# A decoder layer with product-key experts: picks turned at step 14, blocks from step 11, the choice's places and keys in PSUM, half of the first layer norm in PSUM

## The reference, cut to what matters

```python
def reference(x, mem, ...):            # x (1, 512, 1024), one layer
    h = _hybrid_mixer(x, ...)          # gated heads | short convolution, then w_out
    x = _layernorm(ALPHA * x + h, ln1_g, ln1_b)
    h = _cross_attention(x, mem, ...)  # 4 heads over 256 memory tokens
    x = _layernorm(ALPHA * x + h, ln2_g, ln2_b)
    h = _peer(x, ...)
    return _layernorm(ALPHA * x + h, ln3_g, ln3_b)

def _peer(x, w_query, sub_keys, w_down, w_up):      # 128 x 128 experts, each one neuron
    q = (x @ w_query) -> (512 tokens, 8 heads, 2, 128)
    sc = einsum('thpk,hpnk->thpn', q, sub_keys)
    va, ia = top_k(sc[:, :, 0], 16); vb, ib = top_k(sc[:, :, 1], 16)
    top, flat = top_k(va[..., :, None] + vb[..., None, :], 16)   # 16 of the 256 pairs
    expert = ia[flat // 16] * 128 + ib[flat % 16]
    gate = softmax(top)
    act = gelu(sum_d w_down[expert] * x)
    return sum_k gate * act * w_up[expert]
```

## Time and profile before

| | |
|---|---|
| median of 3 runs | 1678.34 us (1678.11 to 1678.65) |
| profiled execution | 1678.76 us, its span 1676.9 us |
| PE, PEld | 93%, 83% of the span busy |
| DVE, ACT, POOL | 73%, 37%, 47% |
| mean granted PE clock | 0.965 of full speed |
| bytes moved | 410.80 MB, 245 GB/s over the span |
| front block, scores, down tiles up to the Gelu of tile 127, up tiles and end | 0 to 396, 396 to 520, to 1134, to 1677 us |

### The profile page before, as it was taken

The page is one execution under the profiler, slowest core; times in us unless marked ns, Lnnn a source line. Parts: engine busy times, 40 slices in busy tenths (PEclk is TensorE's granted clock), DMA queues, the critical chain, the costliest instruction groups (busy, mean ns, idle before and its releaser), DMA issues.

```text
span 1676.9 us, 22738 instructions
## 1 busy us (share of the span) xinstructions
PE 1557.5 (93%) x8252; PEld 1387.2 (83%) x8252; DVE 1218.1 (73%) x2298; ACT 626.2 (37%) x807; POOL 787.0 (47%) x460
## 2 busy tenths in 40 slices
PE   7999979897999879996999699999999999999995
PEld 6787857675889879996999699998888888888884
DVE  2544270416999988887988797468888888888887
ACT  4223232322224326632663366333333333333331
POOL 7443454041345777777768777852222222222220
PEclk9999989897999889998999899999999999999997
DMA  8422222113225768797779777998999999999992
GB/s 290 172 95 80 100 101 91 35 50 151 89 75 177 241 213 270 245 390 301 266 243 406 296 254 262 371 364 319 345 334 345 334 339 337 336 342 331 346 379 85
DMA packets 140232, 410.80 MB, mean 245 GB/s; under 512 B 15200, under 2 KB 49248, under 8 KB 139616
## 3 DMA queue, kind: packets, MB, share of 16 engines
q1 hardware_dynamic: 97072, 253.86, 43.1%
q0 software_dynamic: 36864, 134.23, 22.4%
q10 hardware_dynamic: 6192, 21.32, 3.3%
HBM read 363.22 MB, written 46.14 MB: 244 GB/s over the span
## 4 chain that ended last, share of the span: by engine, by line
PE 56%; DVE 17%; DMA 2%; issue 1%; POOL 0%; ACT 0%; DVEq 0%; ACTq 0%
PE ps L1239 10%; PE ps L1241 10%; PE ps L1240 10%; PE ps L927 7%; PE ps L928 7%; PE ps L929 7%; DVE rows L1259 2%; DMA rows<-in_w_down,expert 2%; PE ps L1211 1%; PE ps L1213 1%; DVE gmat L650 1%; DVE gmat L643 1%; DVE ab L733 1%; DVE gb L724 1%; DVE gmat L644 1%
## 5 line engine op out<-in xcount | busy, mean ns | idle before, releaser
L1119 ACT ACTIVATE w_hi<-raw 128x1024 fp32r<-128x1024 f32 x252 | 266.3, 1057 | 346.3 <-PE ps L1241 322.3
L927 PE MATMUL ps<-b_hi,w_hi 128*128 128x384 f32 x1024 | 349.2, 341 | 8.0 <-POOL w_lo L1086 8.0
L1086 POOL TENSOR_TENSOR w_lo<-raw,w_hi 128x1024 fp32r<-128x1024 f32 x119 | 287.9, 2421 | 121.4 <-ACT w_hi L1119 120.4
L928 PE MATMUL ps<-b_lo,w_hi 128*128 128x384 f32 x1024 | 344.6, 337 | 0.0
L929 PE MATMUL ps<-b_hi,w_lo 128*128 128x384 f32 x1024 | 344.5, 336 | 0.0
L1094 POOL DMA_INDIRECT rows<-in_w_up,expert x128 | 139.3, 1088 | 388.4 <-DVE ps L1293 370.9
L1239 PE MATMUL ps<-w_hi,b_hi 128*128 128x512 f32 x768 | 298.8, 389 | 0.7 <-ACT act_t L1125 0.7
L1241 PE MATMUL ps<-w_hi,b_lo 128*128 128x512 f32 x768 | 298.8, 389 | 0.0
L1240 PE MATMUL ps<-w_lo,b_hi 128*128 128x512 f32 x768 | 298.8, 389 | 0.0
L183 POOL TENSOR_TENSOR w_lo<-raw,w_hi 128x1024 fp32r<-128x1024 f32 x60 | 152.0, 2544 | 202.0 <-ACT w_hi L211 202.0
L1300 DVE TENSOR_TENSOR w_lo<-raw,w_hi 128x1024 fp32r<-128x1024 f32 x133 | 163.0, 1225 | 87.8 <-ACT w_hi L1119 87.8
(11 more groups left out here) (217 smaller groups left out, 2467.8 us busy)
## 6 DMA issues: line engine op xcount, KB each, us to landing
raw<-in_down_t SPq DMA_DIRECT2D x128, 512.0 KB, 4.0
raw<-in_up_t SPq DMA_DIRECT2D x128, 512.0 KB, 5.2
raw<-in_units SPq DMA_DIRECT2D x76, 512.0 KB, 3.2
act_d<-act_t SPq DMA_DIRECT2D x128, 192.0 KB, 5.2
c<-act_d SPq DMA_DIRECT2D x128, 192.0 KB, 5.4
gate_d<-gmat ACTq DMA_DIRECT2D x32, 512.0 KB, 15.1
v<-gate_d SPq DMA_DIRECT2D x16, 512.0 KB, 6.7
i<-gate_d SPq DMA_DIRECT2D x16, 512.0 KB, 6.5
```

Source lines behind the costliest of these rows:

```text
L927: nc.tensor.matmul(out, ring.w_hi[:, s, w], b_hi[:, c, 0:DT], start=c == 0, stop=False)
L928: nc.tensor.matmul(out, ring.w_hi[:, s, w], b_lo[:, c, 0:DT], start=False, stop=False)
L1086: nc.gpsimd.tensor_tensor(w_lo[:, s, :], raw[:, s, :], w_hi[:, s, :].bitcast(F32), ALU.subtract).then_inc(split_done, 1)
L1119: nc.scalar.activation(w_hi[:, u % W4, :], raw[:, u % W4, :], ACT.Copy).then_inc(hi_done, 1)
```

## The change

It has four parts. The first layer norm keeps blocks 0 and 1 in their PSUM banks (sum, statistics and the first operation; the second writes `xres` as before), and DVE makes the low parts of blocks 0 and 1 before the layer norm of block 3. `top_experts` writes the places and a copy of the keys of its block into PSUM bank 5, after a wait for ACT's last read of that bank, and L724 and L729 read one operand there. `LEAD` goes from 9 to 11 and `TURN_TILE` from 12 to 14 (so blocks begin two tiles later, and the picks are turned two tiles later within a block), while the gate rounds stay at steps 16 to 31. Gathers stand one step behind the dot that frees their slot in all steps. The write of `numbers` moves behind the first gates.

```diff
@@ -457,12 +457,19 @@
                 step.up(nc.vector.tensor_tensor(rc[:, 0:n], rc[:, 0:n], nt[:, 0, 0:n], ALU.mult))
                 done()
 
-            def layer_norm(u0, full, turn, ready, order):
+            def layer_norm(u0, full, turn, ready, order, in_bank=(), after=lambda b: None):
+
+                def banks(b):
+                    return ps[:, 2 * b:2 * b + 2, :]
+
+                def wide(x):
+                    return x.rearrange("p (i c) -> p i c", i=2)
 
                 def statistics(b, ready):
                     dve.wait_ge(res_added, ready)
                     for h in range(2):
-                        step.up(nc.vector.bn_stats(bst[:, 2 * b + h, :], xres[:, b, h * HALF:(h + 1) * HALF]))
+                        step.up(nc.vector.bn_stats(bst[:, 2 * b + h, :], ps[:, 2 * b + h, :] if b in in_bank else
+                                                   xres[:, b, h * HALF:(h + 1) * HALF]))
 
                 for i, b in enumerate(order):
                     if i < TB - 1:
@@ -471,7 +478,8 @@
                         dve.wait_ge(unit_done, u0 + KC)
                     for h in range(2):
                         c = slice(h * HALF, (h + 1) * HALF)
-                        added.up(nc.vector.scalar_tensor_tensor(out=xres[:, b, c], in0=xres[:, b, c], scalar=ALPHA,
+                        added.up(nc.vector.scalar_tensor_tensor(out=ps[:, 2 * b + h, :] if b in in_bank else
+                                                                xres[:, b, c], in0=xres[:, b, c], scalar=ALPHA,
                                                                 in1=ps[:, 2 * b + h, :], op0=ALU.mult, op1=ALU.add))
                     if i:
                         statistics(order[i - 1], added.n - 2)
@@ -483,12 +491,14 @@
                 dve.wait_ge(full, 32)
                 for b in range(TB):
 
-                    step.up(nc.vector.scalar_tensor_tensor(out=xres[:, b, :], in0=xres[:, b, :], scalar=mv[:, b, 0:1],
-                                                           in1=lng[:], op0=ALU.subtract, op1=ALU.mult))
+                    x = banks(b) if b in in_bank else wide(xres[:, b, :])
+                    step.up(nc.vector.scalar_tensor_tensor(out=x, in0=x, scalar=mv[:, b, 0:1],
+                                                           in1=wide(lng[:]), op0=ALU.subtract, op1=ALU.mult))
                     done()
 
-                    nc.vector.scalar_tensor_tensor(out=xres[:, b, :], in0=xres[:, b, :], scalar=rc[:, b:b + 1],
-                                                   in1=lnb[:], op0=ALU.mult, op1=ALU.add).then_inc(ready, 1)
+                    nc.vector.scalar_tensor_tensor(out=wide(xres[:, b, :]), in0=x, scalar=rc[:, b:b + 1],
+                                                   in1=wide(lnb[:]), op0=ALU.mult, op1=ALU.add).then_inc(ready, 1)
+                    after(b)
 
             def low_part(lo_, hi_, src, sem_):
                 nc.vector.tensor_tensor(lo_, src, hi_.bitcast(F32), ALU.subtract).then_inc(sem_, 1)
@@ -579,12 +589,20 @@
                     y_low(4 + h - 1)
             y_low(7)
             dve.wait_ge(xres_full, 16)
-            layer_norm(U_MIX, ln1_full, 2, x1_ready, LN1_ORDER)
-            for b in range(TB):
+            def x1_low(b):
                 dve.wait_ge(x1_hi, b + 1)
                 tk = slice(b * P, (b + 1) * P)
                 low_part(a_lo[:, :, tk], a_hi[:, :, tk],
                          ps[:, 2 * (b % 2):2 * (b % 2) + 2, :].rearrange("p a (c j) -> p (a c) j", j=P), x1_split)
+
+            def x1_lows(b):
+                if b == 2:
+                    x1_low(0)
+                    x1_low(1)
+
+            layer_norm(U_MIX, ln1_full, 2, x1_ready, LN1_ORDER, in_bank=(0, 1), after=x1_lows)
+            x1_low(2)
+            x1_low(3)
             for m in range(MB):
                 dve.wait_ge(vhi_done, m + 1)
                 low_part(v_lo[:, m, :].rearrange("p (a n) -> p a n", a=2), v_hi[:, m, :].rearrange("p (a n) -> p a n", a=2),
@@ -656,13 +674,14 @@
 PAIR_ROWS = ((0, 1, 16, 0), (1, 4, 8, 16), (4, 8, 4, 40), (8, 16, 1, 56))
 
 
-def top_experts(nc, step, done, k, b, between):
+def top_experts(nc, step, done, k, b, between, bank_free):
 
 
     top, flat, fi, fif, ab = k["top"], k["flat"], k["fi"], k["fif"], k["ab"]
     c0, c1 = k["c0"], k["c1"]
     ff, fb = k["ab"][:, 0], k["ab"][:, 1]
-    vs, isd = (x[:, bass.ds(b, 1)].rearrange("p o (h s) i -> p (o h) s i", s=2) for x in (k["v16"], k["i16"]))
+    vs = k["v16"][:, bass.ds(b, 1)].rearrange("p o (h s) i -> p (o h) s i", s=2)
+    place, keys = k["place"], k["keys"]
     shape = [P, PH, TOPK, TOPK]
 
     whole0, whole1 = c0, c1
@@ -716,17 +735,21 @@
     done()
     step(nc.vector.tensor_tensor(j, j, fb, ALU.min))
     done()
-    step(nc.vector.tensor_tensor(j, ff, j, ALU.subtract))
+    bank_free()
+    step(nc.vector.tensor_tensor(place[:, 1], ff, j, ALU.subtract))
+    step(nc.vector.tensor_copy(place[:, 0], i))
+    step(nc.vector.tensor_copy(keys.rearrange("p h s i -> p (h s) i"),
+                               k["i16"][:, bass.ds(b, 1)].rearrange("p o u i -> p (o u) i")))
     done()
     between()
     pk = [x.rearrange("p h (k i) -> p h k i", k=TOPK) for x in (whole0, whole1)]
     for side in range(2):
-        step(nc.vector.tensor_tensor(pk[side], fif[:, side].unsqueeze(3).broadcast_to(shape),
+        step(nc.vector.tensor_tensor(pk[side], place[:, side].unsqueeze(3).broadcast_to(shape),
                                      k["iota"][:, 0:TOPK].unsqueeze(1).unsqueeze(1).broadcast_to(shape), ALU.is_equal))
         between()
     done()
     for side in range(2):
-        step(nc.vector.tensor_tensor(pk[side], pk[side], isd[:, :, side, :].unsqueeze(2).broadcast_to(shape), ALU.mult))
+        step(nc.vector.tensor_tensor(pk[side], pk[side], keys[:, :, side, :].unsqueeze(2).broadcast_to(shape), ALU.mult))
         between()
     done()
     for side in range(2):
@@ -904,11 +927,11 @@
 W4 = RING
 ACTS = 4
 ROWS = 4
-LEAD = 9
+LEAD = 11
 BLOCK_TILES = 32
 CHOICE_TILES = 16
 EXP_TILE = 6
-TURN_TILE = 12
+TURN_TILE = 14
 SPLIT_TILE = 120
 ROUNDS = P // RT
 PIECES = 16
@@ -917,6 +940,7 @@
 KEPT = DB - 1
 PB = NK // PIECES
 XB = 6
+PICK_BANK = 5
 
 
 def down_tile(nc, t, ring, s):
@@ -974,6 +998,8 @@
              "fif": sb("fif", [P, 2, PH, TOPK]), "ab": sb("ab", [P, 2, PH, TOPK]),
              "ex": sb("ex", [P, PH, TOPK]), "gsum": sb("gsum", [P, PH]), "iota": sb("iota", [P, P])}
         gate_h = sb("gate_h", [P, PH, TOPK], F16)
+        k["place"] = ps[:, PICK_BANK, 0:2 * HK].rearrange("p (s h i) -> p s h i", s=2, h=PH)
+        k["keys"] = ps[:, PICK_BANK, 2 * HK:4 * HK].rearrange("p (h s i) -> p h s i", s=2, h=PH)
         cols = sb("cols", [P, 4, P], F16)
         rows = sb("rows", [P, ROWS, D])
         expert, gate, dn = t["expert"], t["gate"], t["dn"]
@@ -1023,7 +1049,7 @@
 
         dots = dot_steps()
         tail = LEAD + BLOCK_TILES * DB
-        gathers = [max(LEAD, dots[m - ROWS] + (2 if dots[m] < tail else 1)) if m >= ROWS else LEAD for m in range(HK)]
+        gathers = [max(LEAD, dots[m - ROWS] + 1) if m >= ROWS else LEAD for m in range(HK)]
         halves = 2 * ROUNDS
 
         @block.sync
@@ -1302,8 +1328,7 @@
 
             made = [0]
             dve.wait_ge(const_full, 16)
-            step(nc.vector.tensor_copy(numbers[:], k["iota"][:].unsqueeze(2).broadcast_to([P, P, RJ])))
-            top_experts(nc, step, done, k, GB, lambda: None)
+            top_experts(nc, step, done, k, GB, lambda: None, lambda: None)
             step(nc.vector.scalar_tensor_tensor(out=ef, in0=k["ab"][:, 0].rearrange("p h k -> p (h k)"),
                                                 scalar=float(NK), in1=k["ab"][:, 1].rearrange("p h k -> p (h k)"),
                                                 op0=ALU.mult, op1=ALU.add))
@@ -1311,13 +1336,15 @@
             nc.vector.tensor_copy(expert[:], ef).then_inc(experts_ready, 1)
             dve.wait_ge(exp_out, 1)
             gates(nc, step, done, k, gate[:])
+            step(nc.vector.tensor_copy(numbers[:], k["iota"][:].unsqueeze(2).broadcast_to([P, P, RJ])))
             done()
             dve.wait_ge(xb_ready, 1)
             for b in range(DB):
                 if b:
                     dve.wait_ge(half_done, halves * b)
                 first = made[0]
-                top_experts(nc, step, done, k, b, lambda: dots_until(made[0] + 1))
+                top_experts(nc, step, done, k, b, lambda: dots_until(made[0] + 1),
+                            lambda: dve.wait_ge(half_free, halves * b) if b else None)
                 dve.wait_ge(exp_out, b + 2)
 
                 gates(nc, step, done, k, gparts[:, 0])
```

## The result

The changed kernel takes 1683.45 us (median of 9 runs) where the kernel before takes 1679.07 beside it: ratio 1.0029, 95% interval 1.0020 to 1.0039. It is slower by 0.3%. The forecast was 1621, and its range ended at 1632. All these times are of fast runs. The profiled execution took 1682.49 us.

What follows compares the result with a forecast made beforehand. TensorE, busy 93% of the span, was the bound, so only its waits and slow stretches could be won: 10.9 + 41.1 + 6.8 - 1.5 = 57.3 us off 1678.76 gave 1621.5, as median 1621; range 1615.5 to 1632.

Steps and rivals of the forecast that it cites:

- Part 1: Tile 13 of the first block: LEAD 11 puts two splits ahead of GpSimd's wait for the experts; gains 10.9 us.
- Part 3: The choice's four 128x2048 operations: an operand in PSUM makes each 2.25 us, gaining 2 us per held-up one.
- Part 2: Turns of the picks in three blocks: TURN_TILE 14 removes TensorE's gaps except the transposes; gains 41.1 us.
- Part 4: First layer norm: blocks 0 and 1 in PSUM bring the query product sooner; gains 6.8 us, bounds 0 and 8.1.
- Transfers: Full DMA engines around the gate stores leave splits little margin; costs 1.5 us, bounds 0 and 6 over two blocks.
- The weight ring: Rival: the ring runs dry in blocks 1 and 2, TensorE waits for splits; 15 us, 1636, chance 0.11.
- The tail: After the blocks: 26 rows in 21 tiles instead of 23, 3.4 us a row, costed at nothing.
- What is late next is not on the path: Between turn and first gate round: VectorE's copy and one round take about 4 us of 8.3, margin 4 us.
- The gate rounds become VectorE's: Rival in the gate rounds: VectorE can't get ahead; slower than before only from a 6.35 us cycle; chance 0.03.
- TensorE never waited for a round: Argument about the gate rounds, against the rival that they become VectorE's: TensorE had no such wait before; no size given.

Runs made afterwards that it cites:

- d2: Changed kernel with gathers two steps behind their dot in rounds, three additional dots spread, places and keys back in SBUF: 1677.70 us, ratio 0.9962.
- a3: Kernel before with only the gathers in the blocks asked one step sooner: 1669.78 us, ratio 0.9943.
- a1: Changed kernel with gathers inside the three blocks put back to two steps behind their dot: 1660.83 us, ratio 0.9905.
- c2: Changed kernel with the three additional dots behind round 1 made before the wait for turned picks, gathers as changed: 1656.47 us, ratio 0.9868.
- c1: Changed kernel with the three additional dots made before the wait for turned picks and the rounds' gathers two steps behind their dot: 1645.67 us, ratio 0.9804.
- the longer delay: Kernel before with two needless 128x2048 sums (2.29 us each) after round 4 of block 0: 1687.85 us, ratio 1.0052.
- f1: Changed kernel with TURN_TILE 13 and gathers two steps behind their dot only in the middle of the rounds, one elsewhere: 1654.84 us, ratio 0.9849.

## Why the prediction was wrong, point by point

**The forecast gains came,** as a sum. Stalls ahead of the rounds were to give 57.3 us net and gave 59.6. Their parts were less well seen, and luck has a share.

*Part 1*, 10.9: tiles 12 and 13 are 4.16 apart. But it isn't LEAD's alone. By itself LEAD 11 gave 4.6 us (1674.74 against 1679.31), since TensorE then waits 4.0 us at tile 15, which comes 10.60 us after tile 14; in d2, where the places are back in SBUF, tile 15 comes 10.98 us after tile 14. The 2.3 us of margin forecast at tile 15 were Part 3's 2.2 in the first choice.

*Part 2's turns*, 41.1 with Part 3: the waits at the turns are 0, and tile 25 comes 4.85 us after 24. What the blocks' stalls gave is 12.0 (22.9 less Part 1's 10.9), 14.3 and 14.4 us, against 12.2, 14.5 and 14.4. At the first turn this was luck. The picks were to be 4.5 us early; they were written at 595.92, and TensorE came for them at 595.98:

```profile
595.63 0.29 DVE L1358 TENSOR_TENSOR gparts<-gparts 128x128 f32<-128x128 f32 x1
```

```profile
595.98 0.44 PE L1223 MATMUL ps<-ident,ab 128*128 128x128 f32 x2
```

In block 1 the picks stood at 757.7 (forecast 759.9) and TensorE came 9.0 us later (forecast 8). Counted from the end of block 0's rounds, which itself moved, they came 13.7 us sooner than before, where the prediction had 7 from the gathers and 6 from Part 3. Alone, in a3, the gathers took 5.3 us off that turn's wait, and Part 3 took 2.4 and 4.3 off the waits of blocks 1 and 2. So the total was right and the shares were not; why the two together give more than each alone was not tested.

*Part 3*, four operations at 2.2 to 2.3 us: all 16 took it, beside GpSimd's splits. Rows of L747 and L752, for one side of the two:

```profile
L747 DVE TENSOR_TENSOR gb<-ps,iota 128x2048 f32<-128x2048 f32 x4 | 9.1, 2285 | 0.0
L752 DVE TENSOR_TENSOR gb<-gb,ps 128x2048 f32<-128x2048 f32 x4 | 9.1, 2282 | 0.0
```

*Part 4*, 6.8: operations of blocks 0 and 1 at 1.28, one held (3.30) of those behind, the query product 21.2 us after the first operation (forecast 21.5):

```profile
213.04 1.29 DVE L495 SCALAR_TENSOR_TENSOR ps<-ps,mv,lng 128x1024 f32<-128x1024 f32 x1
...
219.56 3.30 DVE L499 SCALAR_TENSOR_TENSOR xres<-xres,rc,lnb 128x1024 f32<-128x1024 f32 x1
```

```profile
234.22 0.79 PE L305 MATMUL ps<-a_hi,w_hi 128*128 128x512 f32 x1 [2.37 <-DVE a_lo L504]
```

The start of tile 0 moved by 8.0 us between the two profiles, but from execution to execution it moves by up to 4: over the 13 profiles with this part its median is 496.7, over the 7 without 502.4. So the part is worth 5.7 by the profiles (by the runs of the layer norm alone 6.2 from the medians and 4.5 from the ratio, 0.9973), and some 2 of the 8.0 are chance.

*Transfers*, -1.5: no wait for a split tile behind the turns (L951 does not appear among the waits of the changed kernel). The weight ring never ran dry. The tail, costed at nothing, cost nothing: its tiles stay at 4.16. (The ends of the forecast's spread are, by its own terms, 1618 and 1628, not 1617 and 1629; nothing hangs on it.)

**The step that failed** is the last one of Part 2: "What is late next is not on the path". It priced the copy of `cols` and one round at 4 us against 8.3, stopped at round 0, and so put the rounds' own cost at nothing, where they cost 63.4 us. Round 0 was in time, 3.3 us ahead of TensorE in block 0, and round 1 2.1 us; TensorE first waited for round 2 (2.66 us) and then for round 3 (3.50 us). Three things were missing. The copy and round 0 took 7.6 us, not 4, since no split was counted: the round has an `eq_b` of 2.42 and a `gb` of 3.29. The four dots behind round 1, 4.6 us, stand in the code and were not counted; before they lay in the lead of four tiles and the stall. The first of them and the operation behind the last:

```profile
612.18 1.22 DVE L1285 SCALAR_TENSOR_TENSOR rows<-rows,ps 128x1024 f32<-128x1024 f32 x1
...
616.75 0.88 DVE L1372 TENSOR_TENSOR eq_b<-numbers,cols 128x1024 f16<-128x1024 f16 x1
```

And the gathers asked one step sooner were costed as a gain only: the prediction itself asks who is queued behind a moved instruction, but never asked it for the gather in the rounds, which now waits 2.79 us for the dot and takes GpSimd's split with it onto `gb`. Undoing the gathers' step in the rounds gave back 22.6 us (a1), moving the dots 27.0 (c2), both 37.8 (c1); c1 alone has every block open.

**The rival had the mechanism's name and a wrong argument.** "The gate rounds become VectorE's" said slower than before only from a cycle of 6.35 us on; the cycle is 6.38, and the kernel is slower by 4 us. It had 0.03. Against it stood "TensorE never waited for a round". That was true and no evidence, because TensorE's stall at each turn gave VectorE the lead that the change takes away. And the 5.15 of the earlier trace rows was read as what VectorE needs. It is TensorE's beat, handed to VectorE through the split: the need is 3.8 plus the split's uncovered part, and the uncovered part depends on who is late. A term on which two engines agree to 0.01 us may be one that one of them sets for the other.

## What to carry to other kernels

Where two engines run in step, find out who paces whom before pricing the cycle: an equal period can be a lock, and if the follower's work depends on where in the leader's beat a shared resource is taken, one small wait can move it to a slower steady state for good. A stall that is removed was also someone's lead; after it, count everything that its cover held, burst and all, and try the margin by a deliberate delay (2.3 and 4.6 us here) before spending it. Asking for a transfer sooner can move a wait to the engine that asks, and to everything queued behind it.

## What the runs showed of the hardware

- The Trainium skill, "SBUF — State Buffer", section "SBUF: two separate sides", says that the operation which starts first has the shared ports and the other is blocked whole. The runs agree on the blocking: `gb` goes from 0.68 to 3.29 us behind a split of 2.41 and ends 0.55 us after it, so it did its work after the split. On who goes first they don't settle it: the record of that `gb` begins at 646.03, 0.33 us ahead of the split's, and `gb` was the one blocked; but starts of GpSimd's records are rough. The runs add to it: the blocked operation isn't let in between splits issued back to back (8.00 us behind three splits of 7.13).
- The same rounds have at least three steady periods: 5.16 and 5.87 us in one kernel (the longer delay), and 6.38 in f1 next to 5.87, where only the place of the gathers differs.
- After a wait of 2.5 us for round 0 the granted clock of TensorE in c1 is 0.75 of full speed for the round and the tile behind it, part of that time at 1.2 and part at 2.4 GHz, and 1.00 in the tile after; the Gelu comes 9.40 us after its forerunner, not 5.16 (windows view):

```profile
615.30:622.00 6.70, 6.70 (x40) 6.56 (x40) 6.55 (x9) 1.97 (x2) 3.71 (x3) 0.75 0.97 329
622.20:627.30 5.10, 5.10 (x42) 4.94 (x40) 4.97 (x8) 3.38 (x4) 3.41 (x2) 1.00 0.25 81
```

  After the wait of 1.25 us in the kernel with the longer delay it stayed at 1.00.
